# Attention heads in pairs with one normalisation per tile, and the fifth w_mod column block multiplied in the attention instead of in the delta's last round

## The reference, cut to what matters

```python
def softmax_sink(s, sink, groups, rep):                       # windowed attention, 8 heads, 2 key groups
    m = jnp.maximum(jnp.max(s, axis=-1, keepdims=True), sk)
    e = jnp.exp(s - m)
    return e / (jnp.sum(e, axis=-1, keepdims=True) + jnp.exp(sk - m))
...
ob, _, _ = delta_bidir(qb, kb, vb, g, beta, s0_f, s0_b)        # gated delta rule, both directions
...
ob = rmsnorm(ob, out_norm) * jax.nn.silu(gate_b)               # per head of the delta's output
out = jnp.concatenate([oa, ob], axis=-1) @ w_out
...
mod = jax.nn.silu(cvec) @ prm["w_mod"][l] + prm["b_mod"][l]    # (1024) x (1024 x 6144), both layers
```

## Time and profile before

| | |
|---|---|
| median of 3 runs | 1928.52 us (1926.64 to 1929.06) |
| profiled execution | 1928.23 us, its span 1926.4 us |
| PE busy | 1841.1 us, 96% |
| DVE, ACT, POOL busy | 963.8, 827.9, 55.0 us |
| chain that ended last | PE 85%, DVE 6%, ACT 4%, issue 3% |

### The profile page before, as it was taken

How to read it: one execution, slowest core, us unless ns; L and a number is a source line. 1 busy time by engine, 2 the same in 40 slices (tenths; PEclk the granted TensorE clock), 3 DMA queues, 4 the chain that set the end, 5 groups by cost and what they waited for, 6 DMA issues and landing times.

```text
span 1926.4 us, 36263 instructions
## 1 busy us (share of the span) xinstructions
PE 1841.1 (96%) x14824; PEld 1698.8 (88%) x14824; DVE 963.8 (50%) x1613; ACT 827.9 (43%) x1420; POOL 55.0 (3%) x76
## 2 busy tenths in 40 slices
PE   6999998888899999999999999999999999999998
PEld 3999966667799999999999887776899999999997
DVE  4433355556746655235555743344375553255555
ACT  4545422225745544124445653343464441244453
POOL 0000122220000000000000000000000000000000
PEclk9999999998999999999999999999999999999999
DMA  7222366531021223222234311110211232122243
GB/s 284 65 58 66 128 252 221 199 141 51 1 71 44 77 71 87 71 66 68 73 94 140 95 44 32 27 35 28 67 44 55 76 87 78 55 76 76 78 136 115
DMA packets 238723, 170.23 MB, mean 88 GB/s; under 512 B 20139, under 2 KB 230285, under 8 KB 232333
## 3 DMA queue, kind: packets, MB, share of 16 engines
q1 hardware_dynamic: 238604, 168.54, 28.2%
HBM read 165.08 MB, written 3.44 MB: 87 GB/s over the span
## 4 chain that ended last, share of the span: by engine, by line
PE 85%; DVE 6%; ACT 4%; issue 3%; DMA 1%; SPq 0%; ACTq 0%; DVEq 0%
PE ps L2007 46%; PE ps L2083 15%; PE ps L2040 4%; PE ps L2201 3%; PE ps L2708 2%; PE ps L2745 2%; PE ps L2704 2%; PE ps L2398 1%; PE ps L2220 1%; PE ps L2578 1%; PE ps L2451 1%; PE ps L2555 1%; PE ps L2211 1%; PE ps L2028 1%; ACT w_hi L782 1%
## 5 line engine op out<-in xcount | busy, mean ns | idle before, releaser
L782 ACT ACTIVATE w_hi<-w_raw 128x1024 fp32r<-128x1024 f32 (+4 forms) x187 | 198.6, 1062 | 559.6 <-PE ps L2007 436.0
L1366 DVE TENSOR_TENSOR w_lo<-w_raw,w_hi 128x1024 fp32r<-128x1024 f32 (+4 forms) x191 | 234.2, 1227 | 377.2 <-ACT w_hi L782 376.8
L2007 PE MATMUL ps<-h_hi,w_hi 128*128 128x322 f32 x1648 | 381.5, 313 | 3.2 <-ACT conv L972 1.7
L2007 PE MATMUL ps<-h_lo,w_hi 128*128 128x322 f32 x1648 | 380.2, 312 | 0.0
L2007 PE MATMUL ps<-h_hi,w_lo 128*128 128x322 f32 x1648 | 378.1, 310 | 0.0
L2007 PEld LDWEIGHTS ps<-h_hi,w_hi 128*128 128x128 f32 x1648 | 278.1, 189 | 4.8 <-ACT conv L1192 2.0
L2007 PEld LDWEIGHTS ps<-h_hi,w_lo 128*128 128x128 f32 x1648 | 279.1, 189 | 0.0
L2007 PEld LDWEIGHTS ps<-h_lo,w_hi 128*128 128x128 f32 x1648 | 279.1, 189 | 0.0
L2083 PE MATMUL ps<-g_hi,w_hi 128*128 128x322 f32 x352 | 110.7, 314 | 2.7 <-DVE g_lo L1850 1.6
L2083 PE MATMUL ps<-g_lo,w_hi 128*128 128x322 f32 x352 | 109.6, 311 | 0.0
L2083 PE MATMUL ps<-g_hi,w_lo 128*128 128x322 f32 x352 | 109.1, 310 | 0.0
(11 more groups left out here) (376 smaller groups left out, 3337.5 us busy)
## 6 DMA issues: line engine op xcount, KB each, us to landing
w_raw<-in_ffn_w_up SPq DMA_DIRECT2D x88, 512.0 KB, 3.7
w_mod_raw<-in_w_mod SPq DMA_DIRECT2D x40, 1024.0 KB, 6.9
w_raw<-in_ffn_w_down SPq DMA_DIRECT2D x48, 704.0 KB, 4.5
w_raw<-in_ev_w_in SPq DMA_DIRECT2D x18, 512.0 KB, 3.6
w_mod_first<-in_w_mod SPq DMA_DIRECT2D x8, 1024.0 KB, 15.6
w_raw<-in_ev_w_out SPq DMA_DIRECT2D x8, 512.0 KB, 4.3
w_raw<-in_od_w_out SPq DMA_DIRECT2D x8, 512.0 KB, 4.0
w_raw<-in_od_w_kv_up SPq DMA_DIRECT2D x24, 128.0 KB, 2.3
```

The source lines that it names most:

```text
L782: act.activation(WH[slot][:, 0:k, :], RAW[slot][:, 0:k, :], ACT.Copy).then_inc(w_hi, 1)
L1366: dve.tensor_tensor(WL[slot][:, 0:k, :], RAW[slot][:, 0:k, :], WH[slot][:, 0:k, :].bitcast(F32), ALU.subtract).then_inc(w_lo, 1)
L2007: last = pe.matmul(out, w_of(k, wi), x_of(k, xi, i), start=(k == 0 and p == 0), stop=(k == ks - 1 and p == 2))
```

## The change

Delta: round 4 multiplies no pieces (it still transposes the block before), and the eight pieces of the fifth block are multiplied in the attention, two in each of pairs 1 to 4; their transposes and their columns follow at pair 6, in bank 6. Four `keep_busy` matmuls of 256 columns stand after the delta's last product and four more after the first scores.

Attention: PE's loop goes by pairs: scores of pair i, values of pair i-2, transposes of pair i-1. DVE issues both row maxima of a pair together. The sink's exponential, the denominator, the reciprocal and the scaling are done once for the eight units of a tile (`att_scale(i)`, one operation over 512 columns). ACT's copy comes two units behind its exponential instead of one; the steps of a delta head are spread over 14 units instead of 10, and the first weights are split at u = 12 and 13 instead of 2 and 3. `keep_busy` in the last tile is two matmuls a pair instead of one a unit.

```diff
-    ON_AT = [4 + 8 * h for h in range(B_HEADS)]
+    ON_AT = [2 + 8 * h for h in range(B_HEADS)]
+    def a_max_at(u):
+        return S("a_max"), u + 1 + u // 8
...
             # ACT, for each unit u
-                act.wait_ge(S("a_max"), u + 1)
+                act.wait_ge(*a_max_at(u))
                 if u >= 2:
                     act.wait_ge(S("a_turned"), u - 1)
                 act.activation(PR[s][:, c0:c1], SM[s][:, c0:c1], ACT.Exp, ...).then_inc(S("a_exp"), 1)
-                act.activation(ASM[:, 192 + u:193 + u], SNK[:, h:h + 1], ACT.Exp, bias=ASM[:, 64 + u:65 + u]
-                               ).then_inc(S("a_sink"), 1)
-                if u >= 1:
-                    att_copy_a(act, u - 1)
-                if u in (2, 3):
+                if u % 8 == 7:
+                    act.wait_ge(S("a_max"), 9 * (i + 1))
+                    act.activation(ASM[:, 192 + 8 * i:200 + 8 * i], ASM[:, 192 + 8 * i:200 + 8 * i], ACT.Exp, scale=A_HD ** -0.5
+                                   ).then_inc(S("a_sink"), 1)
+                if u >= 2:
+                    att_copy_a(act, u - 2)
+                if u in (12, 13):
...
                 on_step(u)
-                if u % 8 == 3 and t != ATT[0]:
-                    att_out(ATT.index(t) - 1, "oa_hi")
+                if u % 8 == 6 and u > 8:
+                    att_out(u // 8 - 1, "oa_hi")
...
             # DVE: one scaling for a tile
+            def att_scale(i):
+                dve.wait_ge(S("a_sink"), i + 1)
+                den = ASM[:, 8 * i:8 * i + 8]
+                step(dve.tensor_tensor(den, ASM[:, 128 + 8 * i:136 + 8 * i], ASM[:, 192 + 8 * i:200 + 8 * i], ALU.add))
+                step(dve.reciprocal(den, den))
+                dve.wait_ge(S("a_pv"), 8 * (i + 1))
...
+                if u % 8 == 3 and u > 8:
+                    att_scale(i - 1)
+                if u % 8 == 7 and u > 8:
+                    att_lo(i - 1)
+                if u == 11:
+                    mod_rows(MROUNDS - 1)
+                if u == 13:
+                    mod_out(MROUNDS - 1, 6)
...
             # PE, the delta's rounds
-                    for k in range(3):
-                        mod_piece(r, k)
+                    if r < NT - 1:
+                        for k in range(3):
+                            mod_piece(r, k)
+                    else:
+                        pe.wait_ge(S("a_rotated"), r)
+                        mod_turn(r + 1, MROW, 7)
...
+            pe.wait_ge(S("a_rotated"), NT)
+            keep_busy(7, 4)
...
             # PE, the attention
-                if u >= 2:
-                    pe.wait_ge(S("oa_scaled"), u - 1)
+                if i >= 2:
+                    pe.wait_ge(S("oa_scaled"), i - 1)
...
+            for i in range(NPAIR + 2):
+                u = 2 * i
+                if i < NPAIR:
+                    att_scores(u)
+                if i == 0:
+                    keep_busy(7, 4)
+                if i >= 2:
+                    att_values(u - 4)
+                    att_values(u - 3)
+                if 1 <= i <= NPAIR:
+                    att_turn(u - 2)
+                    att_turn(u - 1)
+                if 1 <= i <= KD // 2:
+                    mod_piece(NT - 1, u - 2)
+                    mod_piece(NT - 1, u - 1)
+                if i == 6:
+                    mod_turn(MROUNDS + 1, MROW, 6)
+                on_stat(u)
+                on_stat(u + 1)
...
+                if i >= 18:
+                    keep_busy(7, 2)
+                if i % 4 == 2 and i > 4:
+                    if i == 6:
+                        pe.wait_ge(S("mod_cols"), MROUNDS + 1)
+                    att_out(i // 4 - 1)
```

More of the change, by code:

```diff
@@ L453, in build, with by_unit @@
     A_ROPE = (4, 0, 1, 2, 3)
-    ON_AT = [4 + 8 * h for h in range(B_HEADS)]
+    ON_AT = [2 + 8 * h for h in range(B_HEADS)]
+    NPAIR = len(ALLU) // 2
+    def a_max_at(u):
+        return S("a_max"), u + 1 + u // 8
+    def by_unit(m, i, first=0):
+        return m[:, first + 8 * i:first + 8 * i + 8].rearrange("p (c g) -> p c g", g=2)
     def on_head(u, step):
@@ L1805, in _ @@
                 dve.tensor_scalar(ASM[:, 64 + u:65 + u], ASM[:, u:u + 1], -A_HD ** -0.5, None, ALU.mult).then_inc(S("a_max"), 1)
[L1806 to L1821 removed]
+                if u % 2 == 0:
+                    continue
+                if u % 8 == 7:
+                    dve.tensor_tensor(by_unit(ASM, i, 192), SNK8[:, :].rearrange("p (g c) -> p c g", g=2), by_unit(ASM, i), ALU.subtract
+                                      ).then_inc(S("a_max"), 1)
+                if u % 8 == 3 and u > 8:
[3 more added lines that the diff above has]
+                if u == 11:
+                    mod_rows(MROUNDS - 1)
+                if u == 13:
+                    mod_out(MROUNDS - 1, 6)
+                if u in (13, 15):
+                    w_rest(N0_EVEN_OUT + u // 2 - 6)
+                for x in (u - 1, u):
+                    if 16 <= x < 23:
+                        j = x - 15
+                        gains(j // 4, j // 2 % 2, 1 + j % 2)
+                    on_step(x)
+            att_scale(NT - 1)
             att_lo(NT - 1)
@@ L2314, in mod_piece @@
                 u = KD * r + k
-                if k == 0 and r > 0:
+                if k == 0 and 0 < r < NT - 1:
                     pe.wait_ge(S("a_rotated"), r)
@@ L2438, in _ @@
                         k_times_state(r, lv - 4 - e)
-                    elif r == 0 and lv < 5 or r > 0 and lv < 4:
+                    elif r < NT - 1 and (r == 0 and lv < 5 or lv < 4):
                         mod_first_half(r, lv + 2 * (1 - e))
@@ L2456, in _ @@
                         last.then_inc(S("tr_done"), 1)
-                    if r == 0 and lv < 5 or r > 0 and lv < 4:
+                    if r == NT - 1:
+                        pass
+                    elif r == 0 and lv < 5 or r > 0 and lv < 4:
                         mod_piece(r, lv + 2 * (1 - e), halved=True)
@@ L2481, in _ @@
                     k_times_state(r, 1)
-                else:
+                elif r < NT - 1:
                     mod_first_half(r, LEVELS)
@@ L2571, in att_values @@
                 pe.wait_ge(S("a_pt"), u + 1)
-                if u >= 2:
-                    pe.wait_ge(S("oa_scaled"), u - 1)
-                out = PS[:, (4 + u % 2) * 512 + 64 * h:(4 + u % 2) * 512 + 64 * h + 64]
+                if i >= 2:
+                    pe.wait_ge(S("oa_scaled"), i - 1)
+                out = PS[:, (4 + i % 2) * 512 + 64 * h:(4 + i % 2) * 512 + 64 * h + 64]
                 tiles = att_tiles(t)
```

71 lines of the change are left out of this document (22 added, 49 removed).

## The result

The changed kernel is slower: 1937.28 us median of 7 runs (1933.82 to 1945.56) against 1927.03 us (1926.47 to 1930.49) of the kernel before, a ratio of 1.0047 with a 95% interval of 1.0031 to 1.0062. A second comparison on another chip gave 1936.78 against 1929.49 us, 1.0045 (1.0030 to 1.0061). The forecast was 1920.2.

The account below looks back on a forecast made before the run. PE bounds nearly everywhere, but a chain over three engines bounds the attention. Terms -7.0 - 6.2 + 0.1 + 0.1 + 3 = -10.0, plus 2 us for the clock: -8.0 from 1928.2, so 1920.2 us; range 1916 to 1930.

Parts of the forecast that it names:

- the charge for the clock: Attention: one short fall of PE's clock in the likeliest case, 2 us added to the -10.0 at full clock.
- Part 2: Attention pairs 0 to 3: full clock with pieces and constants filling PE, 15.5 us instead of 21.7, 6.2 us less.
- Part 3: Attention pairs 4 to 15: an ACT-PE loop of 4.4 us plus head work; +0.1 for 4 to 11, +0.1 for 12 to 15.
- Part 1: Delta's round 4 without its pieces: level 0 starts earlier, levels take 2.3 us each; 7.0 us less, bounds 4 and 9.5.
- Rival 1: Attention: the clock falls two or three times and returns, 6 us instead of 2, 1924 us; chance 0.27.
- Rival 2: Attention: the clock falls and stays low through pairs 6 to 15, 16 us on top, 1934 us; chance 0.13.
- the bounds: Round 4's gain: 4 us if 1.9 us of unexplained PE waiting stay and levels take 0.2 more; 9.5 at most.
- Part 4: Attention's last tile: a longer drain, 8.9 us from the last scores against 7.2; +3 us, bounds 1 and 4.

Follow-up runs that it names:

- a_att_only: The changed kernel with round 4 as before: its pieces back there, none in the attention's pairs; 1935.78 us, 1.0035 to the kernel before.
- b_keep: The kernel before with only the change's eight constant matmuls, four behind the delta's last product and four behind the first scores; 1928.93 us, ratio 1.0001.
- a_order: The changed kernel with ACT's work on delta heads and the tile moved behind the odd unit's copy; 1929.39 us, 0.9997 to the kernel before.
- a_alt: The changed kernel with PE alternating per pair: even values, even transposes, odd values, odd transposes; 1920.61 us, 0.9962 to the kernel before.

## Why the prediction was wrong

Four terms failed, three of them of about the same size: the charge for the clock (2 us forecast, 7.4 by the estimate), Part 2 (-6.2, measured -0.8), Part 3 (+0.2, measured +5.4) and Part 1 (-7.0, measured -4.7). So the gain of 10 us was gone before the clock made a loss of it.

**The clock**: "In the likeliest case I charge one short fall, 2 us". It fell in five stretches of the attention in each profile, and over the executions the charge is 7.4 us, a part of it outside the attention (above). I had computed the gaps rightly (1.3 and 1.8 us; 1.11 and up to 1.7 measured). But 1.6 us busy of 3.4, my own number around the longer gap, stands beside the row where the clock fell after 1.54, not beside the one where it stayed after 2.02, and such a gap comes in one pair of four; for charging a single fall I had no reason but the steady clock of the kernel before, in whose pairs 4 to 11 PE waits for 0.9 us at the most. A fall after 2.18 us shows besides that 2.02 is no bound. Rival 1 had the mechanism, several falls and returns, but stood on the same wrong base of -10. The Trainium skill ("TensorE: Matmul & The Clock Gate", section "A second HAM failure mode: psum-queue depth-cycling"), cited against the change, says that a PE idling briefly and often between groups of matmuls swings between its two clocks and loses throughput by it. The trace agrees in kind, with stretches of 3.4 to 13.6 us at half clock between stretches at full; the page's own case, cycling through PSUM banks, no run here tests. Rival 2, a clock that stays low from pair 6 on, did not come.

**Part 2** failed in its baseline. Pairs 0 to 3 take 17.0 us with full clock (forecast 15.5; the four pairs take 2.8, 3.5, 5.6 and 5.1 instead of 2.5, 3.4, 4.8 and 4.8), but the 21.7 us that they were set against were one execution's fall; in the other profile they took 17.8. The gain is 0.8 us, not 6.2. The pieces do not ride for nothing, as `a_att_only` shows, and neither do the constants: each group of four takes 1.9 us on PE, where I had 0.9. Behind the delta that lies mostly in the wait for DVE, 1.42 us; behind the first scores the pair waits anyway for its first exponential. In `b_keep` the first scores come 0.1 us later behind `kq_copy` than in the kernel before.

```profile
432.75 1.89 PE L2224 MATMUL ps<-consts 128*128 128x256 f32 x8
434.58 0.49 PE L2581 MATMUL ps<-qa_ka_va 64*128 64x128 f32 x4
```

**Part 1** had the right mechanism and too large a size: from the end of `kq_copy` to the first scores it is 32.5 us before (405.72 to 438.23) and 28.9 after (405.71 to 434.58), so 3.6 instead of 7.0. The levels gave 5.4 (last addition at 422.13 in the row below, against 427.49). In the 1.5 us between the last additions of the two chains PE waited 0.75 us for nothing that the profile shows, which I had counted among the bounds only, and some 1.1 of what is missing is the clock, which fell between 422 and 430 us in each of the nine profiles of a round 4 without pieces and in none of the six with all of them.

```profile
420.66 0.29 DVE L1719 TENSOR_TENSOR r_blocks<-r_blocks,ps 128x128 f32<-128x128 f32 x1 [0.32 <-PE ps L2476]
422.13 0.29 DVE L1719 TENSOR_TENSOR r_blocks<-r_blocks,ps 128x128 f32<-128x128 f32 x1 [0.99 <-PE ps L2476]
```

**Part 3** named the loop between ACT and PE and what falls into it, and `a_order` and `a_alt` confirm both. Pairs 8 to 11 take 21.1 us by their row maxima, one microsecond of it clock (forecast 20.3). Pairs 4 to 7 take 24.5, not 21.0: pair 6, with the first weight's high half, 8.9 instead of 7.0, and pair 7 6.3 instead of 5.3. What the part missed is the reading: I took the loop as given by the work, while it is given by the order that puts both values ahead of both transposes. The units of the kernel before went transposes, values, transposes, values, which covers the copies; the pairing undid that.

**Part 4** came out by luck: 20.3 us where 20.2 were forecast, but 6.8 us of them at half clock, some 2 us, which the part did not hold. At equal clock it is 18.1, so +0.5 instead of +3. The longer drain is there (from the first row maximum of pair 19 to the end 8.0 us against 6.1 before); the pairs ahead of it are not longer but shorter.

At equal clock the sum is then, an estimate from the second profiles with 0.32 us taken off for each low microsecond (round 4 of the kernel before from the first, which had no fall there): round 4 -4.7, pairs 0 to 3 -0.8, pairs 4 to 11 +3.5, pairs 12 to 15 +1.9, the rest +0.5; +0.4, about nothing in place of -10. With 7.4 us of clock that makes +7.8, against the +7.3 measured in the second comparison and +10.3 in the first.

## What to carry to other kernels

When work is grouped by pairs, interleave on the engine that waits: put the half that is ready between the two halves that wait for another engine. Price a stretch against several executions before a gain is taken from it, above all where its granted clock is below 1. A wait of PE of about a microsecond in every other step cost twice here, as waiting and as clock. Constants that were longer than the wait cost nearly what they saved (5.8 of 7.8 us); reordering cost nothing.

## What was not expected of the hardware

The falls move between executions of the same program: the kernel before ran from 1923.8 to 1937.5 us over 84 executions, with the mean clock between 0.987 and 0.999. PE lost its clock once after it had been busy for 2.18 of the 3.4 us before, and kept it in another place after 2.02 of 3.4. The shortest stretches at half clock in the profiles last 3.4 us, the longer ones in the attention 6.8 to 17.
